# Two-block RWKV-7 and attention layer on one core: key norms and bonus sums spread by DMA

## The chip, the cores and the metric

One core of a Trainium2 chip runs the whole kernel. The metric is the device time of one execution in microseconds (us), lower is better. The time of the kernel before is known from three runs, and one more execution was profiled.

## The reference, cut to what matters

The layer takes x of 512 tokens by 1024 channels. A normed input is multiplied by a wide matrix; from its columns come an RWKV-7 recurrence, a windowed attention and gates, then two projections, an output matrix and a feed-forward block with a short convolution. The change touches the RWKV part alone, in two of its expressions:

```
kk = heads(kf * k_k)
kk = kk / maximum(sqrt(sum(kk * kk, axis=-1)), 1e-12)          # key norms
...
bonus = sum(rh * kh * r_k, axis=-1, keepdims=True) * vh         # bonus sums
y = (groupnorm(y) * lnx_w + lnx_b + bonus) * g
```

Both need a sum over the 64 channels of a head for every token, and then that one number again in all 64 channels.

## The kernel before, in words

Everything is written by hand, one instruction stream for each engine, with semaphores between them. A channel sits in a partition and the 512 tokens run along the row. Sixteen heads go in eight pairs, one pair (n = 0 to 7) filling the 128 partitions; z[:, n] holds r, z[:, n + 8] k and z[:, n + 16] v of pair n. The tokens are four chunks (j) of 128. For each pair TensorE does, in this order:

- scan(n - 1): the state goes over the four chunks of the pair before, and its output lands in bank 6;
- scores(n, n - 1): sixteen 64-row products (L1837) give the chunk matrices; norm_var (L1816) sums the squared output of the pair before over channels with by_row (L1768), four products with 32 columns of weights each that write different 32-row stripes of bank 6; turned_var, deviations and turned (L1776) turn these numbers and spread them over channels; bonus(n - 1) (L1806) multiplies the product r*k in z[:, d + 8] by rkones, a 128x128 matrix of r_k in head blocks, and gives the bonus sum of a head in all its channels in one step;
- invert(n, n - 1) (L1860): seven levels (lv = 0 to 6) that double an inverse of eight 128x128 matrices. A level from 1 on is: PE products L1898 and transposes L1876, DVE masked copies L1355 (v), PE products L1921, DVE sums L1362 (yy), each in two groups. ACT copies the transposed half (L902).

These are short, dependent steps, so PE fills its waits from a table: `fill(place)` runs k-steps of a large fp32r product with the input (three matmuls, L1652 to L1654), "masks" after L1898 and "update" after L1921. Eight steps are one tile of 128 columns of w_in; a pair takes three tiles: FILL = SLOT_A, SLOT_C, SLOT_B (L2010 to L2016). Every tile needs its weights split beforehand in a high part by ACT (L714) and a low part by DVE (L1118, 1024 columns), which DVE does in the levels 1 and 4 of the inversion and at its pair's start.

DVE carries the other pieces of the pair before in the same levels of its own invert (L1332): add_bonus (L1302) at level 2, with_bonus (L1313) and the spreading of the next key norms at level 3, gated (L1318) at level 5. For pairs 0 to 2 fill_low (L1327) is added at levels 3 and 6. scaled_output (L1307) runs ahead of value_tokens (L1252). At its start invert makes xx (L1336) from n1 and the constant first_level, both in SBUF, and level 0 of yy (L1347) follows xx.

The key norms: key_sums (L1782) gathers the sums of all sixteen heads as rows of bank 2, one row for a chunk and head; ACT takes the root into krow (L822); PE turns krow (turned_sums, L1794); DVE takes the reciprocal (L1272). For each pair DVE copies two columns over 64 columns each into kqn (L1279), PE turns kqn (key_norms, L1798), ACT copies it back (L826), and DVE multiplies it in at the start of the next scan (key, L1212).

GpSimd (POOL) has its own queue, in order: the attention's stores, the zeroing of gb and gk, and for each pair bonus_product (L634, r*k of the pair), gate_out (L625, DMA stores), and remainder (L629), which subtracts the two SBUF tensors gb and n1 and is needed at the end of the inversion. kqn lies at the same place as ysq, the spread deviations. SyncE loads weights, each load waiting for the low part three tiles earlier.

Of the kernel before, what the change touches and what calls it, by code (L numbers as in the profile page):

```python
# [36 lines left out]
P = 128  # L37
T = 512
D = 1024
KT = D // P  # L40
# [18 lines left out]

RAW, HL = 4, 2  # L60
# [49 lines left out]
def build(nc, x, norm1_g, w_in, rwkv_mu, w0, w2, a0, a2, g2, k_k, k_a, r_k, lnx_w, lnx_b,  # L110
          b_qkv, attn_sink, gate_b, w_proj_a, w_proj_b, w_out, norm2_g, w_up, conv_w,
          conv_b, w_down, normf_g, out):
    with ExitStack() as ctx:
# [104 lines left out]
        knorm = take("knorm", [P, NT, 2 * PAIRS])  # L218
# [17 lines left out]
        rkones = take("rkones", [P, P])  # L236
        take = taker(KVR, PREP)
# [4 lines left out]
        gk = take("gk", [P, NT, 2, 2 * C])  # L242

# [29 lines left out]
        attn = nc.dram_tensor("attn_scratch", (P, KT, T), F32, kind="Internal").ap()  # L273
        ps = [ctx.enter_context(nc.psum_tensor(f"ps{b}", [P, T], F32)) for b in range(8)]
# [4 lines left out]
        w_hi = sem("w_hi")  # L279
        w_lo = sem("w_lo")  # L280
# [48 lines left out]
        norm_ps = sem("norm_ps")  # L329
        kex_ready = sem("kex_ready")  # L330
        kn_ps = sem("kn_ps")
        kqn_ready = sem("kqn_ready")
# [199 lines left out]
        def _(pool):  # L532
# [125 lines left out]
            for c in (6, 7):  # L658
                attention_out(c)
# [46 lines left out]
        def _(act):  # L706
# [117 lines left out]
            def key_norm_back(n, bank=6):  # L824
                act.wait_ge(kn_ps, n + 1)
                act.activation(kqn[:, :], ps[bank][:, :], ACT.Copy).then_inc(kqn_ready, 1)  # L826

# [66 lines left out]
            def invert(n, d, following):  # L894
# [9 lines left out]
                for lv in range(LEVELS):  # L904
# [11 lines left out]
                    if lv == 5 and following:  # L916
                        key_norm_back(n + 1)
# [34 lines left out]
            for t in range(RKV_TILES):  # L952
# [28 lines left out]
                if t == RKV_TILES - 1:  # L981
                    key_norm_back(0, 2)
# [25 lines left out]
            act.wait_ge(bonus_ps, PAIRS)  # L1008
# [103 lines left out]
        def _(dve):  # L1112
# [93 lines left out]
            def prepare(n):  # L1206
# [5 lines left out]
                def key():  # L1212
                    dve.wait_ge(kqn_ready, n + 1)
# [58 lines left out]
            def key_factors():  # L1272
                dve.wait_ge(norm_ps, 1)
                sums = ps[2][:, P:2 * P].rearrange("p (j h) -> p j h", j=NT)[:, :, 0:2 * PAIRS]
                chain(dve.tensor_scalar(knorm[:, :, :], sums, 1e-12, None, ALU.max))
                chain(dve.reciprocal(knorm[:, :, :], knorm[:, :, :]))

            def key_norms(n):
                dve.tensor_copy(kqn[:, :].rearrange("p (j h v) -> p j h v", j=NT, h=2),  # L1279
                                knorm[:, :, 2 * n:2 * n + 2].unsqueeze(3)  # L1280
                                .to_broadcast([P, NT, 2, HD])).then_inc(kex_ready, 1)
# [20 lines left out]
            def add_bonus(d):  # L1302
                dve.wait_ge(bonus_ps, d + 1)
                dst, bank = (tile(d + 8), 5) if d < PAIRS - 1 else (bp[:, :], 2)
                chain(dve.tensor_tensor(dst, tile(d + 16), ps[bank][:, :], ALU.mult))
# [18 lines left out]
            def weights(n):  # L1324
                split(n, n % RAW, n % HL)

# [5 lines left out]
            def invert(n, d, following):  # L1332
# [7 lines left out]
                for lv in range(LEVELS):  # L1340
# [913 lines left out]
```

## Time and profile before

| | |
|---|---|
| median of 3 runs | 1091.56 us (1091.25 to 1093.53) |
| the profiled execution's own time | 1091.47 us |
| its span on the core | 1089.6 us |
| granted TensorE clock, mean | 0.998 of full speed (2.4 GHz) |
| PE busy | 1072.5 us, 98% |
| DVE busy | 681.1 us, 63% |
| ACT busy | 503.5 us, 46% |
| POOL busy | 99.9 us, 9% |
| DMA | 97.01 MB, 89 GB/s mean |

The profile is of one execution. PE intervals overlap, since matmuls are pipelined: what one costs is the step from its start to the next one's start, not its length. The eight pairs lie between about 225 and 580 us of the span. An idle time in brackets stands before the instruction, with what ended it.

### The profile page before, as it was taken

To read this page: it belongs to the slowest core of one execution; us is meant where nothing else is said; L and a number is where in the kernel's file an instruction comes from. 1 tells how busy PE (TensorE), PEld (TensorE's weight loads), DVE (VectorE), ACT (ScalarE), POOL (GpSimd) and SP (SyncE) were. 2 spreads that over 40 slices of the span, in tenths; PEclk is the share of its full clock that TensorE was granted. 3 is DMA by queue.
4 is the path that set the end of the run, shared out by engine and by line. 5 is a ranking of instruction groups with operands and counts; after the bars stand their busy time and mean duration, and the time that the engine had idled before them with its cause. 6 is when DMAs were issued, how large, how long until landed. Compare 5 with 4: busy or idle time off the path is not lost.

```text
span 1089.6 us, 17946 instructions
## 1 busy us (share of the span) xinstructions
PE 1072.5 (98%) x6737; PEld 847.2 (78%) x6737; DVE 681.1 (63%) x1159; ACT 503.5 (46%) x860; POOL 99.9 (9%) x150
## 2 busy tenths in 40 slices
PE   7999999999999999999999999999999999999997
PEld 6887887777777777777777888888888888888886
DVE  4224655687887878878876445457777776752234
ACT  5426675634534445345443333465555556531122
POOL 8100000120010110111110110100000000000000
PEclk9999999999999999999999999999999999999999
DMA  7632323211101211113242553423333333322221
GB/s 199 154 89 87 96 80 92 74 48 40 40 24 47 78 40 59 59 43 84 80 136 78 155 154 116 135 78 96 96 92 100 88 90 91 96 97 97 97 78 78
DMA packets 154390, 97.01 MB, mean 89 GB/s; under 512 B 30761, under 2 KB 143703, under 8 KB 154327
## 3 DMA queue, kind: packets, MB, share of 16 engines
q1 hardware_dynamic: 148800, 79.72, 25.5%
q0 software_dynamic: 5376, 16.37, 4.7%
q8 instruction: 45, 0.74, 0.3%
q14 instruction: 18, 0.15, 0.0%
q10 hardware_dynamic: 151, 0.04, 0.0%
HBM read 87.71 MB, written 8.39 MB: 88 GB/s over the span
## 4 chain that ended last, share of the span: by engine, by line
PE 94%; DVE 3%; ACT 1%; issue 1%; ACTq 0%; DVEq 0%
PE ps L1696 16%; PE ps L1699 16%; PE ps L1698 16%; PE ps L1652 5%; PE ps L1654 4%; PE ps L1653 4%; PE ps L2213 4%; PE ps L2211 4%; PE ps L2212 4%; PE ps L1837 3%; PE ps L1969 2%; PE ps L1778 2%; PE ps L1990 2%; PE ps L1921 1%; PE ps L1898 1%; PE ps L1876 1%
## 5 line engine op out<-in xcount | busy, mean ns | idle before, releaser
L1118 DVE TENSOR_TENSOR wlo<-raw,whi 128x1024 fp32r<-128x1024 f32 x142 | 173.7, 1223 | 210.4 <-ACT whi L714 138.3
L714 ACT ACTIVATE whi<-raw 128x1024 fp32r<-128x1024 f32 x124 | 131.2, 1058 | 124.3 <-PE ps L1699 120.6
L1696 PE MATMUL ps<-xnh,whi 128*128 128x512 f32 x344 | 135.8, 395 | 0.0
L1699 PE MATMUL ps<-xnh,wlo 128*128 128x512 f32 x344 | 135.7, 395 | 0.0
L1698 PE MATMUL ps<-xnl,whi 128*128 128x512 f32 x344 | 135.7, 395 | 0.0
L1696 PE MATMUL ps<-xh,whi 128*128 128x512 f32 x248 | 99.7, 402 | 1.7 <-DVE xl L1136 1.7
L1699 PE MATMUL ps<-xh,wlo 128*128 128x512 f32 x248 | 97.9, 395 | 0.0
L1698 PE MATMUL ps<-xl,whi 128*128 128x512 f32 x248 | 97.9, 395 | 0.0
L1652 PE MATMUL ps<-xh,whi 128*128 128x512 f32 x184 | 87.0, 473 | 0.0
L1698 PEld LDWEIGHTS ps<-xnl,whi 128*128 128x128 f32 x344 | 64.8, 188 | 15.2
L1696 PEld LDWEIGHTS ps<-xnh,whi 128*128 128x128 f32 x344 | 64.8, 188 | 15.1
L1699 PEld LDWEIGHTS ps<-xnh,wlo 128*128 128x128 f32 x344 | 64.8, 188 | 15.0
L1654 PE MATMUL ps<-xh,wlo 128*128 128x512 f32 x184 | 72.9, 396 | 0.0
L1653 PE MATMUL ps<-xl,whi 128*128 128x512 f32 x184 | 72.2, 392 | 0.0
L902 ACT ACTIVATE xx<-ps 128x256 f16<-128x256 f32 x96 | 32.0, 382 | 79.9 <-PE ps L1876 79.9
L2213 PE MATMUL ps<-wlo,hh 128*128 128x512 f32 x160 | 63.1, 395 | 0.0
L2211 PE MATMUL ps<-whi,hh 128*128 128x512 f32 x160 | 63.1, 394 | 0.0
L2212 PE MATMUL ps<-whi,hl 128*128 128x512 f32 x160 | 63.1, 394 | 0.0
L1696 PEld LDWEIGHTS ps<-xh,whi 128*128 128x128 f32 x248 | 46.6, 188 | 13.9 <-DVE wlo L1118 1.9
L1699 PEld LDWEIGHTS ps<-xh,wlo 128*128 128x128 f32 x248 | 46.6, 188 | 11.1
L1698 PEld LDWEIGHTS ps<-xl,whi 128*128 128x128 f32 x248 | 46.7, 188 | 10.2
L722 ACT ACTIVATE whi<-raw 128x1024 fp32r<-128x1024 f32 x18 | 19.1, 1059 | 73.7 <-PE ps L2213 73.7
(355 smaller groups left out, 2180.1 us busy)
## 6 DMA issues: line engine op xcount, KB each, us to landing
raw<-in_w_in SPq DMA_DIRECT2D x108, 256.0 KB, 3.2
raw<-in_w_up SPq DMA_DIRECT2D x88, 256.0 KB, 3.2
raw<-in_w_down SPq DMA_DIRECT2D x44, 256.0 KB, 2.8
gates_scratch<-gst POOLq DMA_DIRECT2D x16, 256.0 KB, 2.4
raw<-in_w_proj_b SPq DMA_DIRECT2D x16, 256.0 KB, 4.1
raw<-in_w_proj_a SPq DMA_DIRECT2D x16, 256.0 KB, 3.2
gl<-gates_scratch POOLq DMA_DIRECT2D x16, 256.0 KB, 3.1
raw<-in_w_out SPq DMA_DIRECT2D x16, 256.0 KB, 3.1
```

The lines of the kernel that those rows point to most:

```text
L714: act.activation(flat(whi[:, hb]), flat(raw[:, b]), ACT.Copy).then_inc(w_hi, 1)
L1118: dve.tensor_tensor(flat(lo[:, hb]), flat(raw[:, b]), flat(hi[:, hb]).bitcast(F32), ALU.subtract).then_inc(w_lo, 1)
L1652: pe.matmul(o, whi[:, hb, k, :], self.hi(k), start=k == 0, stop=False)
L1653: pe.matmul(o, whi[:, hb, k, :], self.lo(k), start=False, stop=False)
L1654: ins = pe.matmul(o, wlo[:, hb, k, :], self.hi(k), start=False, stop=k == KT - 1)
L1696: pe.matmul(ps[bank][:, :], whi[:, hb, k, :], hi(k), start=first and k == 0, stop=False)
L1698: pe.matmul(ps[bank][:, :], whi[:, hb, k, :], lo(k), start=False, stop=False)
L1699: ins = pe.matmul(ps[bank][:, :], wlo[:, hb, k, :], hi(k), start=False, stop=last and k == kn - 1)
L1837: ins = pe.matmul(ps[SCORE_BANK[f + h]][:, (j - j0) * 2 * C: (j - j0 + 1) * 2 * C], src[hs, j * C:(j + 1) * C], ar[hs, 1 - n % 2, j, :], s ...
L2211: pe.matmul(o, hh[:, u, toks], hi[:, cols], start=u == 0, stop=False)
L2212: pe.matmul(o, hl[:, u, toks], hi[:, cols], start=False, stop=False)
L2213: ins = pe.matmul(o, hh[:, u, toks], lo[:, cols], start=False, stop=last)
```

## The change

The inverse key norms are computed as rows: DVE clamps krow and takes its reciprocal in place (128x128 values), POOL stores the rows once in a scratch tensor in DRAM, and for each pair two DMAs read the row of a head back with a stride of zero over its 64 channels, straight into kqn. turned_sums, the copy L1279, the turns of kqn and ACT's copy L826 go. For pairs 0 to 6 the bonus sums are made in norm_var by a second by_row with rkcols, 32 columns of weights (ACT writes them in the place of rkones), into the upper stripe columns of bank 6; ACT copies them to brow ahead of the root of the variance; POOL stores brow, waits for that store, and issues two DMAs that read the rows back over the channels into z[:, d + 8]. All this stands in POOL's queue between bonus_product and remainder; the load of the next kqn stands behind remainder. add_bonus reads SBUF for both inputs. Pair 7 keeps the old bonus.

On DVE scaled_output goes from ahead of value_tokens to level 2 of the inversion, add_bonus from level 2 to 3, with_bonus from 3 to 4, and the two splits of levels 1 and 4 become halves of 512 columns at levels 1 and 2, and 4 and 5, with a semaphore w_half for tiles that begin before their second half is there. One of the two fill steps at (4, "masks") goes to (4, "update").

```diff
@@ pool @@
+            def by_head(rows, c):
+                return rows.rearrange("(j c) t -> c j t", j=NT)[c:c + 1].to_broadcast([HD, NT, P])
+            def key_norms_in(n):
+                for h in range(2):
+                    pool.dma_start(kqn[h * HD:(h + 1) * HD, :].rearrange("p (j t) -> p j t", j=NT),
+                                   by_head(key_rows, 2 * n + h)).then_inc(kqn_in, 16)
+            def bonus_back(d):
+                pool.wait_ge(std_ready, d + 1)
+                pool.dma_start(bonus_rows, brow[:, :]).then_inc(brow_stored, 16)
+                pool.wait_ge(brow_stored, 16 * (d + 1))
+                for h in range(2):
+                    pool.dma_start(z[h * HD:(h + 1) * HD, d + 8, :]
+                                   .rearrange("p (j t) -> p j t", j=NT),
+                                   by_head(bonus_rows, h)).then_inc(bonus_in, 16)
+            attention_out(6)
+            pool.wait_ge(krow_ready, 1)
+            pool.dma_start(key_rows, krow[:, :]).then_inc(krow_stored, 16)
+            pool.wait_ge(krow_stored, 16)
+            key_norms_in(0)
+            attention_out(7)
...
             pool.memset(zp[:, :], 0.0).then_inc(cleared, 1)
+            key_norms_in(1)
             remainder(0)
...
                     gate_out(3 * n - 1 - FILL_V)
+                bonus_back(n - 1)
                 remainder(n)
+                if n < PAIRS - 1:
+                    pool.wait_ge(rstd_ps, n)
+                    key_norms_in(n + 1)
@@ scalar @@
-            def key_norm_back(n, bank=6):
...
             def deviation(d):
                 act.wait_ge(var_ps, d + 1)
+                if d < PAIRS - 1:
+                    act.activation(brow[:, :], ps[6][:, P:2 * P], ACT.Copy)
...
-                        act.activation(rkones[:, :], headones[:, :], ACT.Copy, scale=pcol("rk", n))\
+                        dst, src = (rkcols, keycols[:, KEY0:KEY0 + P // NT]) if following else \
+                            (rkones, headones[:, :])
+                        act.activation(dst[:, :], src, ACT.Copy, scale=pcol("rk", n))\
@@ vector @@
-                    dve.wait_ge(kqn_ready, n + 1)
+                    dve.wait_ge(kqn_in, 32 * (n + 1))
...
             def key_factors():
-                dve.wait_ge(norm_ps, 1)
...
+                dve.wait_ge(norm_ready, 1)
+                chain(dve.tensor_scalar(krow[:, :], krow[:, :], 1e-12, None, ALU.max))
+                dve.reciprocal(krow[:, :], krow[:, :]).then_inc(krow_ready, 1)
...
             def add_bonus(d):
+                if d < PAIRS - 1:
+                    dve.wait_ge(bonus_in, 32 * (d + 1))
+                    chain(dve.tensor_tensor(tile(d + 8), tile(d + 16), tile(d + 8), ALU.mult))
...
+            def weights_half(n, half):
+                ks = slice(half * KT // 2, (half + 1) * KT // 2)
+                if half == 0:
+                    dve.wait_ge(w_hi, n + 1)
+                last = dve.tensor_tensor(flat(wlo[:, n % HL, ks]), flat(raw[:, n % RAW, ks]),
+                                         flat(whi[:, n % HL, ks]).bitcast(F32), ALU.subtract)
+                last.then_inc((w_half, w_lo)[half], 1)
@@ vector, invert @@
-                    if lv == 1 and d is not None:
-                        weights(N_FILL + 3 * n + 1)
+                    if lv in (1, 2) and d is not None:
+                        weights_half(N_FILL + 3 * n + 1, lv - 1)
                     if lv == 2 and d is not None:
-                        add_bonus(d)
-                    if lv == 3 and d is not None:
-                        with_bonus(d)
+                        scaled_output(d)
                     if lv == 3:
-                        if following:
-                            key_norms(n + 1)
+                        if d is not None:
+                            add_bonus(d)
                         fill_low(3 * n)
                     if lv == 4:
-                        weights(N_FILL + 3 * n + 2)
+                        if d is None:
+                            weights(N_FILL + 2)
+                        else:
+                            with_bonus(d)
+                            weights_half(N_FILL + 3 * n + 2, 0)
                     if lv == 5 and d is not None:
+                        weights_half(N_FILL + 3 * n + 2, 1)
                         gated(d)
...
                 for f in range(6, 8):
                     masked(n, f)
-                scaled_output(n - 1)
                 value_tokens(n)
@@ tensor @@
             def norm_var(d):
...
-                by_row(6, ysq, meancols[:, :]).then_inc(var_ps, 1)
+                last = by_row(6, ysq, meancols[:, :])
+                if d < PAIRS - 1:
+                    pe.wait_ge(rk_product, d + 1)
+                    pe.wait_ge(rk_ready, d + 1)
+                    last = by_row(6, z[:, d + 8, :], rkcols[:, :], P)
+                last.then_inc(var_ps, 1)
...
-                if d is not None:
-                    bonus(d)
...
-                    if lv == 5 and following:
-                        key_norms(n + 1)
...
-            SLOT_C = {(2, "update"): 1, (3, "masks"): 1, (4, "masks"): 2, (5, "masks"): 2,
-                      (5, "update"): 1, (6, "masks"): 1}
+            SLOT_C = {(2, "update"): 1, (3, "masks"): 1, (4, "masks"): 1, (4, "update"): 1,
+                      (5, "masks"): 2, (5, "update"): 1, (6, "masks"): 1}
```

## Rows read from the trace of the kernel before

**Rows 1.** The profile's page: busy shares, and the chain's shares by engine.
```profile
PE 1072.5 (98%) x6737; PEld 847.2 (78%) x6737; DVE 681.1 (63%) x1159; ACT 503.5 (46%) x860; POOL 99.9 (9%) x150
...
PE 94%; DVE 3%; ACT 1%; issue 1%; ACTq 0%; DVEq 0%
```

**Rows 2.** The chain in order of time, pair 5's scores and level 1: start, us, what.
```profile
450.82 0.86 PE ps L1809 x2
...
456.25 1.13 DVE wlo L1118
```

**Rows 3.** Timeline of PE, same pair: start, length, engine, line, operation.
```profile
446.67 0.43 PE L1772 MATMUL ps<-ysq,meancols 128*32 128x128 f32 x8
...
457.77 0.62 PE L1921 MATMUL ps<-v,xx 128*128 128x64 f16 x8 [0.15 <-DVE v L1355]
458.23 0.48 PE L1652 MATMUL ps<-xh,whi 128*128 128x512 f32 x1
...
459.01 0.29 PE L1898 MATMUL ps<-yy,n 128*128 128x64 f16 x4
...
459.49 0.48 PE L1652 MATMUL ps<-xh,whi 128*128 128x512 f32 x1
```

**Rows 4.** Timeline of DVE in the inversion of the same pair.
```profile
452.04 0.68 DVE L1336 TENSOR_TENSOR xx<-n,first_level 128x1024 f16<-128x1024 f16 x1
...
457.30 0.74 DVE L1355 TENSOR_TENSOR v<-ps,level_mask 128x256 f16<-128x256 f32 x2
458.10 0.75 DVE L1362 TENSOR_TENSOR yy<-ps,yy 128x256 f16<-128x256 f32 x2
458.78 0.68 DVE L1305 TENSOR_TENSOR z<-z,ps 128x512 f32<-128x512 f32 x1
459.49 0.76 DVE L1355 TENSOR_TENSOR v<-ps,level_mask 128x256 f16<-128x256 f32 x2
...
462.05 0.43 DVE L1279 COPY kqn<-knorm 128x512 f32<-128x512 f32 x1
...
467.26 0.68 DVE L1321 TENSOR_TENSOR z<-ysb,ps 128x512 f32<-128x512 f32 x1
467.85 0.74 DVE L1355 TENSOR_TENSOR v<-ps,level_mask 128x256 f16<-128x256 f32 x2
```

**Rows 5.** Timeline ahead of the first pair: PE and DVE around its key norms.
```profile
214.88 0.66 PE L1778 MATMUL ps<-ident,kqn 128*128 128x128 f32 x4
...
215.29 0.48 PE L1696 MATMUL ps<-xh,whi 128*128 128x512 f32 x1
...
217.51 0.74 DVE L1214 SCALAR_TENSOR_TENSOR kkn<-z,par,kqn 128x512 f32<-128x512 f32 x1
```

**Rows 6.** Timeline of ACT: the root of the variance, in the same scores.
```profile
447.16 0.37 ACT L856 ACTIVATE yrow<-ps,eps_col 128x128 f32<-128x128 f32 x1 [2.83 <-PE ps L1772]
```

**Rows 7.** Timeline of POOL: its product alone, then in a later pair; DMA issues; remainder.
```profile
217.89 0.84 POOL L623 DMA_DIRECT2D attn_scratch<-q  x1 [13.80 <-DVE q L1441]
...
226.25 1.27 POOL L638 TENSOR_TENSOR z<-z,kmod 128x512 f32<-128x512 f32 x1
...
442.60 2.11 POOL L638 TENSOR_TENSOR z<-z,kmod 128x512 f32<-128x512 f32 x1 [16.35 <-DVE kp L1247]
444.67 0.58 POOL L627 DMA_DIRECT2D gates_scratch<-gst  x1
448.57 2.25 POOL L631 TENSOR_TENSOR n<-gb,n 128x1024 f16<-128x1024 f32 x1 [3.32 <-ACT n L885]
```

**Rows 8.** DVE beside POOL: the split at 442 us; L1219's durations (ns, min/median/max).
```profile
442.37 1.22 DVE L1118 TENSOR_TENSOR wlo<-raw,whi 128x1024 fp32r<-128x1024 f32 x1
...
L1219 DVE TENSOR_SCALAR t<-t x8: 415/416/824, 218.2 to 519.8; 128x512 f32<-128x512 f32 x8
```

**Rows 9.** DMA issues on the page: count, KB each, median us from issue to landing.
```profile
gates_scratch<-gst POOLq DMA_DIRECT2D x16, 256.0 KB, 2.4
...
out<-ot SPq DMA_DIRECT2D x1, 192.0 KB, 2.3
```

More of the change, by code:

```diff
@@ L57 @@
 NEG = -1e30
+KEY0 = 2 * PAIRS * 2 - 2
 RAW, HL = 4, 2
@@ L236, in build @@
         rkones = take("rkones", [P, P])
+        brow = take("brow", [P, P])
         take = taker(KVR, PREP)
@@ L242, in build @@
         gk = take("gk", [P, NT, 2, 2 * C])
+        rkcols = take("rkcols", [P, P // NT])
         yah = at(XHL, "yah", [P, KT, T], F32R)
@@ L273, in build @@
         attn = nc.dram_tensor("attn_scratch", (P, KT, T), F32, kind="Internal").ap()
+        key_rows = nc.dram_tensor("key_scratch", (P, P), F32, kind="Internal").ap()
+        bonus_rows = nc.dram_tensor("bonus_scratch", (P, P), F32, kind="Internal").ap()
         ps = [ctx.enter_context(nc.psum_tensor(f"ps{b}", [P, T], F32)) for b in range(8)]
@@ L328, in build @@
         norm_ready = sem("norm_ready")
[L329 to L332, printed above, removed]
+        krow_ready = sem("krow_ready")
+        krow_stored = sem("krow_stored")
+        kqn_in = sem("kqn_in")
+        brow_stored = sem("brow_stored")
+        bonus_in = sem("bonus_in")
         tanh_ready = sem("tanh_ready")
@@ L1272, in key_factors @@
             def key_factors():
-                dve.wait_ge(norm_ps, 1)
[L1274 to L1281, printed above, removed]
+                dve.wait_ge(norm_ready, 1)
+                chain(dve.tensor_scalar(krow[:, :], krow[:, :], 1e-12, None, ALU.max))
+                dve.reciprocal(krow[:, :], krow[:, :]).then_inc(krow_ready, 1)
             def deviations(d):
@@ L1302, in add_bonus @@
             def add_bonus(d):
-                dve.wait_ge(bonus_ps, d + 1)
-                dst, bank = (tile(d + 8), 5) if d < PAIRS - 1 else (bp[:, :], 2)
-                chain(dve.tensor_tensor(dst, tile(d + 16), ps[bank][:, :], ALU.mult))
+                if d < PAIRS - 1:
+                    dve.wait_ge(bonus_in, 32 * (d + 1))
+                    chain(dve.tensor_tensor(tile(d + 8), tile(d + 16), tile(d + 8), ALU.mult))
+                else:
+                    dve.wait_ge(bonus_ps, 1)
+                    chain(dve.tensor_tensor(bp[:, :], tile(d + 16), ps[2][:, :], ALU.mult))
             def scaled_output(d):
@@ L1638, in _, with __init__ @@
             class Tile:
-                def __init__(self, n, bank, hi, lo, free):
+                def __init__(self, n, bank, hi, lo, free, half=None):
                     self.n, self.bank, self.hi, self.lo, self.free, self.k = n, bank, hi, lo, free, 0
+                    self.half = half
                 def __call__(self, count):
@@ L1648, in __call__ @@
                         k = self.k
+                        if k == 0 and self.half:
+                            pe.wait_ge(w_half, self.half)
+                        if k == (KT // 2 if self.half else 0):
+                            pe.wait_ge(w_lo, n + 1)
                         if k == 0:
-                            pe.wait_ge(w_lo, n + 1)
                             pe.wait_ge(ps_free, self.free)
@@ L1766, in small_products, with by_row @@
                               stop=True).then_inc(lora_ps, 1)
-            def by_row(bank, src, sums):
+            def by_row(bank, src, sums, o=0):
                 for j in range(NT):
                     r = j * (P // NT)
-                    ins = pe.matmul(ps[bank][r:r + P // NT, 0:C], sums, src[:, j * C:(j + 1) * C],
-                                    start=True, stop=True)
+                    ins = pe.matmul(ps[bank][r:r + P // NT, o:o + C], sums,
+                                    src[:, j * C:(j + 1) * C], start=True, stop=True)
                 return ins
@@ L1792, in key_sums @@
                 ins.then_inc(ss_ps, 1)
-            def turned_sums():
-                pe.wait_ge(norm_ready, 1)
-                pe.transpose(ps[2][:, P:2 * P], krow[:, :], ident[:, :]).then_inc(norm_ps, 1)
-            def key_norms(n, bank=6):
-                pe.wait_ge(kex_ready, n + 1)
-                turned(bank, kqn).then_inc(kn_ps, 1)
             def deviations(d):
@@ L2039, in following @@
                         free = N_FILL + (t, t - 2, t - 1)[t % 3] if t else N_FILL - 2
-                        self.tile = Tile(N_FILL + t, FILL_BANK[t % 3], xs(xh), xs(xl), free)
+                        self.tile = Tile(N_FILL + t, FILL_BANK[t % 3], xs(xh), xs(xl), free,
+                                         2 * (t // 3) - 1 if t % 3 == 1 and t > 1 else None)
                     else:
@@ L2095, in _ @@
                     small_products(0, (3, 4))
-                if t == RKV_TILES - 1:
-                    key_norms(0, 2)
-                product(n, t % 2, t % 2, xs(xh), xs(xl), tile_n=n,
-                        ready=(lambda k: turned_sums() if k == 4 else None)
-                        if t == RKV_TILES - 2 else None)
+                product(n, t % 2, t % 2, xs(xh), xs(xl), tile_n=n)
             pe.wait_ge(o_done, 8)
```

15 lines of the change are left out of this document (3 added, 12 removed).

## The prediction

> **What bounds the kernel now.** I read the page first: PE is busy 98% of the span, and the chain that ended last runs 94% over PE and 3% over DVE [rows 1]. So time is saved by work taken off PE, unless something else then ends its waits last. The chain in order of time shows where DVE already does: in a pair the bonus product is on it with 0.86 us, and then the split of level 1 with 1.13 us [rows 2]. The timelines say why. In a level DVE and PE form a loop. From L1921 to L1362 are 0.33 us, L1362's two products take 0.68 until the next piece, and the first half of L1355 (0.38) with 0.09 to PE releases the next L1921: 457.30 + 0.38 + 0.09 = 457.77 [rows 3, 4]. That is 1.48 us plus DVE's pieces. PE's own side is L1921 0.25 (half of the sixteen L1898 and L1876, 459.01 to 459.49), a fill step of 0.78 (458.23 to 459.01), 0.48 and a fill of 0.78: 2.29 us [rows 3]. **Pieces over 0.81 us in a level with two fills stall PE**, and then its second group too, by 0.25 (DVE 0.37 for a group, PE 0.12). The split of 1.13 us does so at level 2: 0.32 + 0.25, some 0.55 us.
>
> **The change part by part,** against the profiled execution's own 1091.5 us, which the median of 1091.56 meets within 0.1. It repeats by pair: 0 is special, 1 and 2 have fill_low, 3 to 6 are plain, 7 has no next one.
>
> *Bonus on PE, pairs 1 to 7.* The product of 0.86 us goes [rows 2]. Four more striped products in norm_var come. The trace has the like: eight records in 0.43 us, of which the last's own length is about 0.28 [rows 3]. So they cost between 0.15 and 0.43, and 0.86 if stripes did not run side by side; I take 0.22, nearest to the row. ACT then does a copy of 128 columns ahead of the root, which took 0.37 [rows 6]; back to back I take 0.2 to 0.27 for it. PE hides that behind the "scores" fill but for 0.1. Gain: 0.86 - 0.22 - 0.1 = 0.55 us a pair.
>
> *Levels, pairs 3 to 6.* A 512-column piece takes 0.59 to its successor (467.26 to 467.85), a chained one 0.71 (458.78 to 459.49) [rows 4]. Level 1: half a split, 0.60, no stall: +0.55. Level 2: half a split and scaled_output, 1.31 against 0.81: 0.50 + 0.25, so -0.75. Level 3 has the gate on PE and stays covered. Level 4: the turn of kqn goes (four transposes, 214.88 to 215.29, some 0.42 [rows 5]), with a short wait behind it: +0.55; with_bonus and half a split, 1.38, are covered by the fill moved to "update" and the two after it. Level 5: half a split and gated, 1.19 against 0.81: 0.38 + 0.25, so -0.6. With 0.55 of the bonus: 0.55 + 0.55 - 0.75 + 0.55 - 0.6 = **0.3 us gained a pair**, 1.2 for four. The copy to kqn, 0.43 long [rows 4], is gone from DVE, but two halves cost 0.07 more than a whole split and scaled_output enters the loop: DVE has become the bound.
>
> *Pairs 1, 2.* fill_low at level 3 meets one fill fewer ahead of L1921: 0.3 lost, so 0. *Pair 7:* no turn of kqn to remove: 0.3 lost. *Pair 0:* the turn (0.42) and the wait for DVE's copy (0.3) go: 0.7 gained. *Ahead of it:* the turn of kqn 0.41 and of krow 0.1: 0.5 gained, if kqn comes in time. krow's root lands near 208.7; clamp and reciprocal of 128 columns about 1.3, store 2.0, two issues 1.3, landing of the second 3: 216.5, a microsecond before L1214 needs it at 217.51 [rows 5]. Later loads of kqn are issued behind remainder, some 20 us ahead of their use: nothing. bonus_in lands about 6 us after the root; add_bonus asks for it 12.8 us after: nothing. In the queue of SP nothing is moved; low halves come up to 2 us later, and its loads are tiles ahead.
>
> These sum to -0.5 - 0.7 - 1.2 + 0.3 = -2.1 us: **1089.4 without the next part.**
>
> *What waits behind the store.* The three DMAs stand ahead of remainder on POOL. Now remainder runs beside copies from PSUM at 448.57, for 2.25 us [rows 7]. Count from the root's end. POOL: 0.09, store L, two issues of 0.62 each (between 0.58 for gates_scratch and 0.84 for eight times 256 bytes a partition [rows 7]), so remainder starts at L + 1.35. DVE: turn and reciprocal 0.4, spread 0.6, two masked copies 1.27, vsum 0.72, vp 0.61: xx at 3.6 (now at 452.04; 0.24 later by ACT and the stripes, 0.71 earlier without scaled_output). L is not in the trace: 256 KB from POOL took 2.4, 192 KB from SP 2.3 [rows 9]. A quarter of it in as many rows lies between 1.7 and 2.3; I take 2.0, since size moves little. **Then remainder starts at 3.35, a quarter microsecond ahead of xx.**
>
> Both read two SBUF tensors, and the trace shows what that does. bonus_product took 1.27 us alone and 2.11 when it began 0.23 us into the split at 442.37: it waited out the 1.22 us [rows 7, 8]. The other way round L1219, 0.416 us seven times, took 0.824 when it began at 218.17 inside POOL's issue of 217.89, which lasted 0.84 [rows 7, 8]. By these rows the later one stands until the earlier ends. xx would end 0.26 + 0.26 us behind remainder (L1219 ended 0.26 behind the issue for 0.42 of work; xx is 0.68 long): 3.35 + 2.1 + 0.52 = 5.97 instead of 4.28, 1.7 us late. Little absorbs it: L1347's second product ends 0.09 before PE comes to L1898. So 1.6 us a pair, seven times: +11.2.
>
> The Trainium skill, SBUF — State Buffer, section Who interferes with whom, says the same more strongly: a DVE instruction with two SBUF inputs contends with a GpSimd instruction that reads SBUF, and whoever starts first holds the ports for its whole instruction. It speaks against putting remainder behind a wait of uncertain length. The Trainium skill, DMA: Bandwidth & Descriptors, section Anatomy of one DMA, puts a POOL-issued DMA at about 2.0 us plus its bytes over 436 KB/us, by its estimate 2.15 us for 64 KB; remainder would then start at 3.5, still 0.1 ahead, and the sum would hardly change.
>
> Sum: 1091.5 - 2.1 + 11.2 = **1100.6 us**.
>
> **The rivals.**
> - *Remainder misses xx (1089.4).* It decides at L = 2.25: above that, xx is first, remainder waits 0.7 us, and runs until about 454.6 where level 1 needs only PSUM inputs; the half split begins near 455.7. For it: the margin is 0.25 us, and the row for 256 KB, 2.4, lies above the point. Against: a quarter of the bytes. Or the pair of readers does not exclude each other in this order; only DVE's other kind of instruction shows it. Chance 0.34; of it 0.19 faster, 0.15 within 0.2%.
> - *Some pairs collide (1094 to 1098).* The margin is as small as a store's scatter. Chance 0.10, slower.
> - *PE stays the bound (1083).* 0.64 x 7 of bonus, 0.42 x 8 of turns: 7.9 us, all kept. For it: PE's 98%. Against: level 2 and 5 above, where DVE's pieces exceed 0.81. Chance 0.08, faster.
> - *It trades evenly (1091.5):* halves dearer than 0.60, stripes at 0.43: each 0.1 a pair. Chance 0.03.
> - *All pairs collide:* 0.45, slower, with its own range 1098 to 1102.5 (L from 1.7 to 2.2 gives 1.3 to 1.8 a pair).
>
> That the work does not leave PE at all can't be: the instructions are gone.
>
> **How the numbers follow.** 0.2% (2.2 us) is about what a measurement of this kernel tells from no change. Faster 0.19 + 0.08 = 0.27; same 0.15 + 0.03 = 0.18; slower 0.45 + 0.10 = 0.55. The range from 1088.0 to 1102.5 holds nearly all of the collision, the mixed cases and most of the rival at 1089.4; it leaves out PE as the bound and the tails.
>
> **What the profile after would show.** Right: remainder starts before L1336; L1336 lasts some 2 us, or starts late; L1898 of level 1 waits for DVE by over a microsecond; pairs repeat every 45.4 us instead of 44.1. The rival: L1336 stays at 0.68 us, remainder comes after it, periods near 43.8. In both, stalls of L1921 at levels 3 and 6 and none at level 2. Wrong altogether: add_bonus or L1214 waiting for a DMA, striped products over 0.8 us, or no stall at levels 3 and 6, which would mean that a half split is cheaper than 0.6 us.

## The result and the profile after

The changed kernel takes 1109.97 us (median of 4 runs, 1108.66 to 1110.44), the kernel before beside it 1091.42: a ratio of 1.0164, 95% interval 1.0151 to 1.0176. So it is slower, as forecast, but by 18.5 us and not by 9; 1109.97 lies above the range that ended at 1102.5.

The profile's page of the changed kernel answers to [rows 1]: the chain that ended last has lost six points of PE and gained five of DVE, and among its lines xx, L1372, stands with 2% (the old L1336).

```profile
span 1108.1 us, 18000 instructions
...
PE 1077.0 (97%) x6746; PEld 848.7 (77%) x6746; DVE 695.0 (63%) x1165; ACT 500.2 (45%) x859; POOL 121.5 (11%) x188
...
PE 88%; DVE 8%; issue 2%; ACT 1%; DMA 1%; SPq 0%; DVEq 0%; ACTq 0%
```

PE is busy 4.5 us *longer* than before, though the bonus products and turns are gone from it. That is the first sign that its own steps have become slower.

The timelines of POOL, DVE and PE in pair 5 (452.74 to 499.90 us) answer to [rows 7], [rows 4] and [rows 3]. Columns: start, length, engine, line, operation, and the idle time before it with its releaser.

```profile
458.35 0.54 POOL L676 DMA_DIRECT2D bonus_scratch<-brow  x1 [2.96 <-ACT yrow L888]
460.43 1.25 POOL L679 DMA_DIRECT2D z<-bonus_scratch  x2 [1.54 <-DMA bonus_scratch<-brow]
461.70 2.15 POOL L637 TENSOR_TENSOR n<-gb,n 128x1024 f16<-128x1024 f32 x1
```

```profile
461.06 0.69 DVE L1289 SCALAR_TENSOR_TENSOR vp<-vsum,ps 128x512 f32<-128x512 f32 x1
461.66 2.75 DVE L1372 TENSOR_TENSOR xx<-n,first_level 128x1024 f16<-128x1024 f16 x1
464.33 1.27 DVE L1383 TENSOR_TENSOR yy<-ps,level_mask 128x512 f16<-128x512 f32 x2
```

```profile
465.07 0.29 PE L1932 MATMUL ps<-yy,n 128*128 128x64 f16 x4 [1.29 <-DVE yy L1383]
465.66 0.29 PE L1932 MATMUL ps<-yy,n 128*128 128x64 f16 x4 [0.30 <-DVE yy L1383]
465.79 0.53 PE L1693 MATMUL ps<-xh,whi 128*128 128x512 f32 x1
466.12 0.63 PE L1694 MATMUL ps<-xl,whi 128*128 128x512 f32 x1
466.54 0.63 PE L1695 MATMUL ps<-xh,wlo 128*128 128x512 f32 x1
466.97 0.65 PE L1955 MATMUL ps<-v,xx 128*128 128x64 f16 x8
```

Two things are to be seen. The collision is there: remainder (L637) starts while xx is at work, and xx takes 2.75 us instead of 0.68; it ends 0.56 behind remainder's end (464.41 against 463.85), and PE stands 1.29 us before level 1 (below, this wait is "the gap"). And behind that gap PE's own steps grow: L1694 takes 0.63 us where it took 0.39, and follows its neighbour by 0.42 instead of 0.23. The granted clock says why. Windows of the changed kernel, from one bonus product of POOL to the next (pairs 1 to 6). Columns: the stretch and its length, the busy time of PE, PEld, DVE, ACT and POOL, the granted clock, the DMA share and GB/s:

```profile
264.60:312.21 47.61, 45.21 (x417) 33.50 (x415) 39.92 (x86) 18.85 (x38) 7.28 (x7) 0.96 0.22 47
312.21:359.84 47.63, 45.26 (x423) 33.77 (x421) 39.27 (x85) 19.27 (x39) 7.84 (x9) 0.96 0.24 52
359.84:407.00 47.16, 44.99 (x423) 33.66 (x421) 37.96 (x83) 19.19 (x39) 8.92 (x10) 0.96 0.26 64
407.00:452.74 45.74, 43.42 (x423) 32.57 (x421) 37.92 (x83) 19.05 (x39) 8.91 (x10) 1.00 0.27 66
452.74:499.90 47.16, 44.99 (x423) 33.56 (x421) 37.93 (x83) 19.11 (x39) 8.88 (x11) 0.96 0.27 64
499.90:547.06 47.16, 44.98 (x423) 33.76 (x421) 37.97 (x83) 22.17 (x42) 10.48 (x14) 0.96 0.37 97
```

Five of the six have 0.96 and one has 1.00. In pair 5 the clock is at 0.50, that is 1.2 GHz, from about 466.1 to 469.5, a microsecond behind the gap, and from 469.5 on at 1.00 again. A plain pair (3 to 6) costs 47.16 us with the fall and 45.74 without: **1.42 us for each fall**. The pair without one, 4, has the longest gap of the six, 1.43 us against 1.29 to 1.33.

Where the 18.5 us of the profiled executions (1108.1 against 1089.6 of span) come from, by the starts of POOL's bonus product; the kernel before takes 44.09 to 44.23 us for a pair:

| stretch | predicted change | measured |
|---|---|---|
| up to pair 1 | -1.2 | -1.31 |
| pairs 1, 2 | +1.6 each | +3.39, +3.40 |
| pairs 3 to 6 | +1.3 each | +3.03, +1.63, +3.07, +3.06 |
| pair 7 and the rest | +1.9 | +2.23 |

The pair whose clock held took 1.63 more, near the 1.3 of the prediction.

### The profile page after: what moved, and what is told of

The parts are those of the page before. It is cut to its first block, busy times and chain, and to the rows that moved or that the text cites. A ratio compares the mean times of both kernels' runs of the same rounds, so it can differ in the third digit from the quotient of the medians.

```text
span 1108.1 us, 18000 instructions
## 1 busy us (share of the span) xinstructions
PE 1077.0 (97%) x6746; PEld 848.7 (77%) x6746; DVE 695.0 (63%) x1165; ACT 500.2 (45%) x859; POOL 121.5 (11%) x188
## 4 chain that ended last, share of the span: by engine, by line
PE 88%; DVE 8%; issue 2%; ACT 1%; DMA 1%; SPq 0%; DVEq 0%; ACTq 0%
PE ps L1737 16%; PE ps L1740 16%; PE ps L1739 16%; PE ps L1693 4%; PE ps L2241 4%; PE ps L2242 4%; PE ps L2240 4%; PE ps L1695 3%; PE ps L1694 3%; PE ps L1875 3%; PE ps L2002 2%; DVE xx L1372 2%; PE ps L2023 2%; PE ps L1955 2%; PE ps L1932 1%
## 5 line engine op out<-in xcount | busy, mean ns | idle before, releaser
L1149 DVE TENSOR_TENSOR wlo<-raw,whi 128x1024 fp32r<-128x1024 f32 x128 | 156.7, 1224 | 211.3 <-ACT whi L748 139.1
L1694 PE MATMUL ps<-xl,whi 128*128 128x512 f32 x184 | 74.0, 402 | 0.0
```

What stands on the lines that cost most here:

```text
L1149: dve.tensor_tensor(flat(lo[:, hb]), flat(raw[:, b]), flat(hi[:, hb]).bitcast(F32), ALU.subtract).then_inc(w_lo, 1)
L1694: pe.matmul(o, whi[:, hb, k, :], self.lo(k), start=False, stop=False)
```

## The experiments

All edits but those named otherwise are on the changed kernel. Lines differ by one or two where an edit adds some.

**Where remainder stands on POOL.** Three orders take the collision away, each by other means. x_start is the semaphore that xx raises when it has ended.

```
e1_ahead                e2_after_xx                          e3_store_late
-  bonus_back(n - 1)       bonus_back(n - 1)                 -  bonus_back(n - 1)
   remainder(n)         +  pool.wait_ge(x_start, n + 1)         remainder(n)
+  bonus_back(n - 1)       remainder(n)                      +  pool.wait_ge(x_start, n + 1)
                                                             +  bonus_back(n - 1)
```

> The changed kernel, with remainder (the POOL subtraction n2) queued ahead of the bonus store and its two reads instead of behind them, pairs 1 to 7. Theory (remainder holds xx, and the gap that this leaves on TensorE is followed by a stretch at the lower clock): remainder then starts near 459, right after ACT's n1, beside copies from PSUM as in the kernel before; xx is 0.7 us long again, TensorE waits under 0.6 us before level 1, the granted clock of a pair is 1.00 instead of 0.96. Pairs repeat every 44 instead of 47.2 us, so 1088 to 1092 us; the upper end if the issue of the store, which then comes just ahead of xx, holds xx by some 0.3 us a pair. Rival 1 (DVE is simply the bound after the change, and what xx waits for has come later by its pieces): xx may be short, but the gap before level 1 stays over 1 us and the time stays above 1104. Rival 2 (the DMAs' own traffic delays DVE or TensorE): stays near 1110.

> The changed kernel with one wait more on POOL: remainder starts only when xx has ended (pairs 1 to 7), store and reads stay ahead of it. Theory (remainder holds xx): xx 0.7 us, remainder from about 462.4 to 464.5 beside products out of PSUM, granted clock 1.00, 1088 to 1091 us. If a POOL subtraction with two SBUF inputs also slows DVE's products of PSUM by an SBUF mask, yy would be longer and the time 1092 to 1100. Rival (DVE's backlog, not remainder, is what holds level 1): no more than 3 us below the changed kernel, above 1104.

> The changed kernel with remainder ahead of the bonus store, and the store waiting until xx has ended: neither remainder nor an issue of a DMA stands beside xx. Theory: 1088 to 1090 us, the lowest of the three orders, since add_bonus asks for the sums 12 us after the store; xx 0.7 us, clock 1.00. Rival (DVE's backlog): above 1104, as in the other two orders. If it is over 1 us below the order with remainder ahead alone, the issues hold xx as well.

Measured: 1090.02, 1090.09 and 1089.88 us, ratios to the kernel before 0.9981 (0.9972 to 0.9991), 0.9986 (0.9976 to 0.9995) and 0.9986 (0.9976 to 0.9996). Each gives back all 18.5 us and a little more; the prediction's sum without a collision was 1089.4. xx is 0.68 or 0.69 us long in all three, and a plain pair of e3_store_late:

```profile
397.14:440.83 43.69, 43.12 (x423) 32.51 (x421) 35.73 (x83) 19.05 (x39) 8.94 (x10) 1.00 0.28 69
```

43.69 against 45.74 with the collision and a full clock: the collision costs 2.05 us a pair, the lower clock 1.42 more. DVE's backlog and the traffic of the reads fall as causes, since both are unchanged here. In e1_ahead the store is issued just ahead of xx, beside vp, and nothing is held by it that can be measured.

e3_store_late was expected to be the lowest of the three; its median is lower by 0.14 us only, which is no difference that can be told. With the store issued so late, add_bonus waits for its sums in pairs 1 and 6, by 0.38 and 0.75 us. These two pairs take 44.55 and 44.29 us, against 44.06 and 43.70 in e1_ahead. The row of DVE in pair 6:

```profile
503.38 0.69 DVE L1331 TENSOR_TENSOR z<-z 128x512 f32<-128x512 f32 x1 [0.75 <-DMA z<-bonus_scratch]
```

**Who wins when they meet.** In the changed kernel xx was recorded ahead of remainder in each of pairs 1 to 7, by 0.04 to 0.17 us, and lost each time. Pair 4 has the widest lead; its rows of DVE and of POOL:

```profile
415.92 2.88 DVE L1372 TENSOR_TENSOR xx<-n,first_level 128x1024 f16<-128x1024 f16 x1
```

```profile
416.09 2.15 POOL L637 TENSOR_TENSOR n<-gb,n 128x1024 f16<-128x1024 f32 x1
```

Here remainder waits for vp, the instruction of DVE ahead of xx.

```
                bonus_back(n - 1)
+               pool.wait_ge(vp_ready, n + 1)
                remainder(n)
```

> The changed kernel, with remainder waiting for vp, the DVE instruction ahead of xx: both become ready within about 0.1 us and xx, which follows vp on its own engine, should be first. In the changed kernel itself xx was recorded 0.04 us ahead of remainder and was held all the same, so which of the two wins at such a distance is open. If the one that starts first holds the other in both directions (the row on which the prediction rested): xx stays at 0.7 us, remainder is recorded at up to 2.8 us, 1089 to 1091 us. If remainder holds xx even when it starts at the same time or after it: xx 2.5 us or more, 1105 to 1112 us. If they share, each longer by half: 1093 to 1098 us.

Measured: 1088.60 us, ratio 0.9975 (0.9965 to 0.9985). The rows of DVE and of POOL, pair 5:

```profile
449.40 0.68 DVE L1373 TENSOR_TENSOR xx<-n,first_level 128x1024 f16<-128x1024 f16 x1
```

```profile
449.57 2.52 POOL L637 TENSOR_TENSOR n<-gb,n 128x1024 f16<-128x1024 f32 x1
```

xx is ahead by 0.17 us and keeps its 0.68; remainder takes 2.52 instead of 2.14, so now it is POOL that waits, at no cost. It holds in both directions that one of the two keeps the other out. The recorded starts don't say which: xx lost with leads of 0.04 to 0.17 us in the changed kernel and of 0.21 in e4_fill_in_gap, and won with 0.17 to 0.25 here. What differs is what remainder starts behind, the issue of a DMA there and the semaphore of vp here; that this is the reason is not shown. (By the Trainium skill, SBUF — State Buffer, section Who interferes with whom, issue order decides who blocks the other: the trace agrees that either can be the one held, with 2.75 us one way and 2.52 the other.)

**The collision alone, with no DMA.** On the kernel before, remainder is made to start beside vp.

```
                chain(dve.tensor_reduce(vsum[:, :], ..., ALU.add))
+               dve.memset(carrier[:, 0:1], 0.0).then_inc(summed, 1)
                dve.scalar_tensor_tensor(vp[...], ...)
...
+               pool.wait_ge(summed, n + 1)
                remainder(n)
```

> The kernel before, with no DMA of the change in it: only remainder is made to wait until DVE has summed the values (a small memset behind vsum signals it), so that it starts some 0.4 us ahead of xx. If remainder beside xx and the gap that follows are the whole cause of the loss: xx about 2.4 to 2.8 us instead of 0.68, TensorE waits 1.3 to 1.8 us before level 1, and the granted clock falls to 1.2 GHz behind it in most pairs. 7 x 1.7 us for the wait and up to 7 x 1.4 us for the clock: 1103 to 1112 us. Without the clock falling (only the wait) 1103. Rival (the loss needs the store, the reads or their traffic): within 3 us of the kernel before.

Measured: 1100.82 us, ratio 1.0091 (1.0074 to 1.0108); plain pairs take 45.40 us, 1.3 more than before.

```profile
456.95 2.26 DVE L1339 TENSOR_TENSOR xx<-n,first_level 128x1024 f16<-128x1024 f16 x1
```

```profile
456.53 2.13 POOL L632 TENSOR_TENSOR n<-gb,n 128x1024 f16<-128x1024 f32 x1 [6.36 <-DVE carrier L1260]
```

xx again ends 0.55 behind remainder (459.21 against 458.66), but remainder began 0.42 ahead instead of beside it, so xx is 1.58 late and PE's gap is 0.69 us. The clock stays at 1.00 in every pair: 7 x 1.3 us, and little more. The collision needs none of the change's DMAs. The fall of the clock that was expected with it did not come, and the time lies 2 us below the lower end expected.

**The fall of the clock.** First the gap is filled, with the collision left as it is.

```
-  (0, "masks"): 2, (1, "masks"): 1, (1, "update"): 1, (2, "masks"): 1}
+  (0, "masks"): 3, (1, "masks"): 1, (1, "update"): 1}
```

> The changed kernel with one fill step of slot A moved from (2, masks) to (0, masks), that is into the gap that TensorE has before level 1; the order on POOL and DVE stays, so xx is still held for about 2.7 us. If the stretch at the lower clock follows from the long gap: the gap shrinks from 1.3 to about 0.5 us, a second wait of up to 0.8 us opens at level 2, the sum of the waits stays, but the granted clock of a pair is 1.00 instead of 0.96, and six pairs give back 1.4 us each: 1100 to 1103 us. Rival (the clock falls for another reason, such as power or the count of products): clock still 0.96 in these pairs, 1108 to 1112 us.

Measured: 1102.45 us, ratio 1.0095 (1.0079 to 1.0112). xx is still 2.8 us long (2.94 in pair 5), the gap in pair 5 is 0.79, a wait of 0.39 opens at level 2, and:

```profile
401.99:447.52 45.53, 43.69 (x423) 32.76 (x421) 37.94 (x83) 19.05 (x39) 8.89 (x10) 1.00 0.27 66
```

One k-step of one product in another place gives back 7.5 us. Then gaps are made in the kernel before by DVE alone: xx is written several times over.

```
+               for _ in range(3):        # e12_xx_three_times: 2, e14_xx_six_times: 5
+                   chain(dve.tensor_tensor(xx, n1, first_level, ALU.mult))
                dve.tensor_tensor(xx, n1, first_level, ALU.mult).then_inc(x_start, 1)
```

> The kernel before, with xx written four times over on DVE (three chained copies of the instruction in front of the real one, some 0.71 us each): no DMA and no work on POOL is moved, only xx ends 2.1 us later, in all 8 pairs. The wait alone: 2.05 us a pair, 16 us, 1108. If the clock falls behind the gap by itself, as after the gaps of 1.3 us in the changed kernel: 1.4 us more in most pairs, 1115 to 1120 us, with 1.2 GHz in the 3 to 4 us behind the gap. If what fell there came from the traffic of the reads or from POOL's subtraction: the clock stays at 2.4 GHz, 1107 to 1109.

> As e11_xx_four_times with two copies in front: xx ends 1.4 us later, TensorE waits about 1.3 us before level 1, the same as in the changed kernel (1.29). The wait alone: 8 pairs by 1.35 us, 10.8 us, 1102. If a gap of this length is enough for the clock to fall, as it was in five of six pairs of the changed kernel: up to 10 us more, 1108 to 1113. If the clock stays at 2.4 GHz: 1101 to 1103, and then the changed kernel's fall needed something beside the gap.

Measured: 1109.06 us (1.0166, 1.0148 to 1.0184) and 1101.90 us (1.0101, 1.0083 to 1.0119). Without a fall a pair takes 46.02 and 45.27 us, 1.9 and 1.2 more than before, near the 2.2 and 1.4 by which xx is later. But the gaps that the rows show are 1.27 and 0.54 us (an idle time in them starts at the modelled end of the last matmul, and the second group of products waits 0.30 more), so e11_xx_four_times, not e12_xx_three_times, is the one like the changed kernel. With 0.54 the clock is 1.00 in all six pairs; with 1.26 to 1.30 it fell in one of six:

```profile
267.91:315.06 47.15, 45.53 (x415) 34.04 (x413) 39.90 (x88) 19.26 (x38) 4.39 (x3) 0.96 0.12 35
```

So such a gap can do it without a collision and without a DMA of the change, but need not. Four more experiments ask what decides.

```
e13_mended_xx_four: e1_ahead, xx four times over      e14_xx_six_times: kernel before, six times
e15_changed_shifted: the changed kernel, +  for _ in range(0 if n else 5):   (pair 0 alone)
e16_xx_four_shifted: kernel before,      +  for _ in range(3 if n else 8):
```

> The changed kernel with remainder ahead of the store (no collision), and xx written four times over on DVE, so that TensorE waits some 1.3 us before level 1. If the clock's fall needs the collision or the traffic beside the gap: 1.00 in the pairs, 44.0 + 1.9 = 45.6 to 46 us each, 1104 to 1106. If it follows from the changed kernel's own TensorE work and the gap: 0.96 in most pairs and 1.4 us more each, 1111 to 1115.

> The kernel before with xx written six times over: the gap on TensorE is 1.42 us longer than with four, about 2.7 us. If length decides, the clock falls in all pairs: 46.0 + 1.4 + 1.4 = 48.9 us each, 1128 to 1132. If the moment decides, only in some of them; without any fall, 47.4 us each, 1120.

> The changed kernel, with xx written six times over in pair 0 alone, so that all later pairs come 2 to 4 us later than they did. If the collision, its traffic or the work decides, the clock falls in the same five pairs by the same amount, 1112 to 1114. If the moment decides, another number of pairs falls: 1104 to 1114.

> The kernel before with xx four times over in pairs 1 to 7 and nine times in pair 0: gaps of 1.27 us as in e11_xx_four_times, all of them some 3.5 us later in time. If the moment decides, the clock can fall in other pairs than there, or in more or fewer of them: 1110 to 1120. If not, it is 3.5 us above e11_xx_four_times, 1112.5, with one pair of six at 0.96.

Measured, two runs each: 1115.87 us (1.0222, 1.0192 to 1.0252), 1129.57 (1.0347, 1.0308 to 1.0387), 1114.99 (1.0214, 1.0159 to 1.0269) and 1113.97 (1.0205, 1.0175 to 1.0234). e13_mended_xx_four, with no collision (remainder ahead, xx never held) and gaps of 1.40 to 1.42 us, has 0.96 in five of pairs 1 to 6: the collision is not needed. In e15_changed_shifted the gaps in pairs 1 to 6 are those of the changed kernel (1.29 to 1.42 us) and come 2.5 to 7 us later in time. In the profiled execution two of the five pairs that fell there fall again, 5 and 6, and pairs 1, 2 and 3 keep their clock:

```profile
409.55:455.29 45.74, 43.44 (x423) 32.56 (x421) 37.90 (x83) 19.06 (x39) 8.89 (x11) 1.00 0.27 66
455.29:502.76 47.47, 45.03 (x423) 33.74 (x421) 37.93 (x83) 19.25 (x39) 8.88 (x11) 0.96 0.26 64
```

e16_xx_four_shifted has the gaps of e11_xx_four_times, later in time, on the kernel before, and pair 2 is hit in place of pair 1. Even gaps of 2.7 us (e14_xx_six_times) left two of six pairs at 1.00. So the length of a gap alone doesn't decide: of those from 1.26 to 2.75 us some were followed by a fall and some not, and none up to 0.79 us was, in the profiled executions.

That the moment decides is not shown by this. The number of falls also differs between executions of one and the same kernel. The other execution of e15_changed_shifted took 1117.51 us at a mean clock of 0.987, the profiled one 1112.47 at 0.992: at 1.42 us a fall, an estimate of three falls more with nothing moved. For the changed kernel it is 1108.66 us at 0.994 against 1109.8 to 1110.44 at 0.991. With one profiled execution of each kernel, the shift can't be told from this variation; besides, it was made by a long gap in pair 0 that was followed by a fall itself.

**The levels.** The prediction's steps at levels 2 and 5 are tested by moving halves of the split, on e3_store_late.

```
e7_half_lv6                                   e8_halves_lv3_lv6: the same, and
   if lv == 5 and d is not None:              -  if lv in (1, 2) and d is not None:
-      weights_half(N_FILL + 3 * n + 2, 1)    -      weights_half(N_FILL + 3 * n + 1, lv - 1)
       gated(d)                               +  if lv == 1 and d is not None:
   if lv == 6:                                +      weights_half(N_FILL + 3 * n + 1, 0)
+      if d is not None:                      ...
+          weights_half(N_FILL + 3 * n + 2, 1)          add_bonus(d)
       fill_low(3 * n + 1)                    +         weights_half(N_FILL + 3 * n + 1, 1)
```

> The changed kernel with the store behind xx (the order of e3_store_late), and the last half of the split of tile 3n+2 moved from level 5 to level 6. It tests the prediction's step at level 5: half a split and gated, 1.19 us against an allowance of 0.81, stall TensorE by 0.6 us a pair at level 6. If so, that stall goes, level 6 takes 0.6 us in an allowance that has no other piece in pairs 3 to 7, and 6 pairs give 0.5 us: 1086 to 1088 us. If DVE's pieces do not set the levels (TensorE is the bound as in the rival at 1083): no change, 1089.5 to 1090.5. If the remainder fill then waits for the late half: 1090 to 1094.

> As e7_half_lv6, and the second half of the split of tile 3n+1 moved from level 2 to level 3, beside the gate on TensorE. It tests the prediction's step at level 2 (half a split and scaled_output, 1.31 against 0.81: 0.5 + 0.25 = 0.75 us a pair): scaled_output alone, 0.6 us, should not stall; level 3 then has 1.31 us behind a gate of 1.10 us and may lose 0.1 to 0.4 us of it, and pairs 1 and 2, with fill_low at level 3, lose what they gain. Net 4 x 0.4 to 0.6 us below e7_half_lv6: 1084 to 1086.5 us. If neither level was set by DVE, 1089.5 to 1090.5.

Measured: 1087.15 us (0.9963, 0.9951 to 0.9976) and 1088.43 us (0.9973, 0.9961 to 0.9984). Moving the half out of level 5 takes 0.54 us off a plain pair, 43.15 against 43.69: the 0.6 of the prediction was there. Moving the other out of level 2 does what was expected at its place (from level 3's first group on PE to level 4's 2.57 us instead of 3.16), but level 3 takes all of it back (the next stretch grows from 2.28 to 2.86): 43.10 us a pair, and pairs 1 and 2, with fill_low there too, lose. Two pieces beside the gate are too many: 1084 to 1086.5 was expected, and e8_halves_lv3_lv6 is not even below e7_half_lv6. Both carry the late store of e3_store_late, and add_bonus waits for its sums in pairs 1 and 6 (0.28 and 0.43 us in e7_half_lv6, 0.51 and 0.95 in e8_halves_lv3_lv6); that is part of the loss.

**The key norms alone**, on the kernel before: store and loads of the key rows as in the change, no turn, no spread, no copy back; the bonus stays on PE.

```
+            key_norms_in(0)          # and (1) ahead of remainder(0), (n + 1) behind remainder(n)
-                        if following:
-                            key_norms(n + 1)        # DVE, level 3
-                    if lv == 5 and following:
-                        key_norms(n + 1)            # PE; and ACT's copy back
```

> The kernel before with the key norms' part of the change alone: rows stored to DRAM once, kqn loaded by broadcasting reads on POOL, no turn, no spread copy, no copy back; the bonus stays on TensorE, splits, scaled_output and fills stay as they were, and nothing stands ahead of remainder. By the prediction's terms: turn of kqn with its short wait 0.55 us in each of pairs 1 to 6, 0.7 in pair 0, 0.5 ahead of the pairs: 4.5 us, so 1087 us. If TensorE has no slack to lose in level 4 only the 0.42 us of the turn counts: 1088. If the copy on DVE was hidden and the turn as well: 1091.5. If the loads of kqn hold an instruction of DVE: over 1091.5.

Measured: 1090.31 us, 0.9987 (0.9978 to 0.9996): faster by 1.3 us, not by 4.5. The start gives its part (pair 1's bonus product comes at 265.13 instead of 265.91), but the pairs give none: 44.10 us as before. The timeline of PE, where the turn stood between level 4 and 5:

```profile
462.36 0.41 PE L1913 MATMUL ps<-v,xx 128*128 128x64 f16 x8
463.17 0.29 PE L1890 MATMUL ps<-yy,n 128*128 128x64 f16 x4 [0.40 <-DVE yy L1367]
```

The turn had stood in a wait for DVE's yy, and that wait of 0.40 us is now empty. What it could be worth together with the fill that the whole change moves to (4, "update"), and with the split cut in halves, no run shows.

**Both mends together:** e7_half_lv6 with the order of e6_beside_xx.

> The changed kernel with both mends: remainder waits for vp, so that it starts just behind xx (the order of e6_beside_xx, which had the lowest time of the three orders), and the last half split sits at level 6 (e7_half_lv6). The two act on different waits, so their gains should add: 1088.6 less the 2.7 us that e7 gained on its own base is 1086 us, range 1085 to 1087.5. If the moved half collides with what follows in this order, it stays at 1087 to 1088.6.

Measured: 1087.73 us, 0.9963 (0.9949 to 0.9977). The sum was expected at 1086, and 1087.73 is no better than e7_half_lv6 alone: the two gains do not add where it can be measured. In the profiled execution they do in part: add_bonus waits nowhere, pairs 1 and 6 take 43.49 and 43.16 us against 43.87 and 43.38, and the span is 0.6 us shorter, within what executions of e9_combined differ by (1086.53 to 1088.29). Either is 0.37% below the kernel before and 2% below the changed one.

## Why the prediction was wrong

**The start** (-1.2 us): right, -1.31. But kqn was not there a microsecond early. DVE waited 0.51 us for the load, and key began at 217.38, where it had begun at 217.51. The broadcasting reads landed 4.7 us behind their issue (median), where 3 had been taken. add_bonus never waited for its sums in the changed kernel.

**Bonus on PE** (0.55 gained): from POOL's bonus product to level 1 e3_store_late takes 10.88 us, the kernel before 11.53: 0.65. The second group of stripes started 0.24 us behind the first, against 0.22 taken.

**Levels**, by the first group of L1898 in each (L1933 in e3_store_late), timelines of pair 5 before and in e3_store_late:

```profile
456.20 0.29 PE L1898 MATMUL ps<-yy,n 128*128 128x64 f16 x4
...
461.46 0.28 PE L1898 MATMUL ps<-yy,n 128*128 128x64 f16 x4
...
464.21 0.29 PE L1898 MATMUL ps<-yy,n 128*128 128x64 f16 x4
...
467.28 0.29 PE L1898 MATMUL ps<-yy,n 128*128 128x64 f16 x4
```

```profile
453.78 0.29 PE L1933 MATMUL ps<-yy,n 128*128 128x64 f16 x4
...
456.07 0.29 PE L1933 MATMUL ps<-yy,n 128*128 128x64 f16 x4
...
459.25 0.28 PE L1933 MATMUL ps<-yy,n 128*128 128x64 f16 x4
...
461.52 0.29 PE L1933 MATMUL ps<-yy,n 128*128 128x64 f16 x4
...
464.60 0.29 PE L1933 MATMUL ps<-yy,n 128*128 128x64 f16 x4
```

| from level | before | e3_store_late | gain | predicted |
|---|---|---|---|---|
| 2 to 3 (DVE's piece in level 1) | 2.81 | 2.29 | 0.52 | 0.55 |
| 3 to 4 (level 2) | 2.45 | 3.18 | -0.73 | -0.75 |
| 4 to 5 | 2.75 | 2.27 | 0.48 | 0.55 |
| 5 to 6 | 3.07 | 3.08 | -0.01 | 0 |
| 6 to the decay product (level 5) | 1.60 | 2.11 | -0.51 | -0.6 |

With the 0.65 that is 0.40 a pair, the 44.10 less 43.69 that was measured, against 0.3. For level 4 the reason given was not borne out: e10_keys_only shows that the turn by itself is worth nothing there, so the 0.48 comes from it only together with what else the change does there, or from the rest alone.

**The store.** L, from the store's issue to the end of the wait for it, was 2.08 us (458.35 to 460.43), against 2.0 taken. By the Trainium skill, DMA: Bandwidth & Descriptors, section Anatomy of one DMA, an estimate of 2.15 had been worked out; the trace agrees within 0.1. What was mis-sized is the small term in front of it: the store was issued 0.30 us behind the root's end (457.69 + 0.36), not 0.09. So remainder stood at 3.65 behind the root, not 3.35, and xx at 3.61 (3.6 had been said). By the prediction's own rule xx then comes first and is not held. It was held in all seven pairs, in pair 4 even with a recorded lead of 0.17 us. The mechanism was the one forecast, but by the prediction's own rule it should have missed with the times that were measured: that it came is luck, and a chance of 0.45 against 0.34 was a fair account of it.

**The size of the collision.** xx ended 0.56 behind remainder (0.52 had been said). As remainder began 0.3 later behind the root, xx came out 2.07 us late instead of 1.7, and a pair lost 2.05 instead of 1.6.

**The step that failed** is the price of the collision, "1.7 us late ... So 1.6 us a pair": it ended with PE's wait. The gap of 1.3 us was followed in five pairs by 3.4 us at 1.2 GHz, 1.42 us each. The sum of the first table's excess over the prediction is 3.6 in pairs 1 and 2, 5.6 in pairs 3 to 6 and 0.3 behind, less 0.1 in front: 9.4 us, just what 1109.97 less 1100.6 is; 5 x 1.42 = 7.1 of it is the clock, the other 2.3 the larger collision, 0.45 a pair, less the 0.1 a pair that the levels and the bonus gave beyond the forecast. Without the falls that is an estimate of 1102.9, against 1102.5 where the range ended. The rows of before could not show this, for in its pairs PE has no such gap; but the prediction priced a gap on PE at its length and did not ask what may follow it, and the range had nothing in it for that.

The rivals: the one without a collision, 1089.4, is what e1_ahead, e2_after_xx and e3_store_late are, within 0.7 us. PE as the bound (1083) is excluded by the levels. What stays open is what decides whether the clock falls behind a gap, and why e6_beside_xx came out 1.3 to 1.5 us below the other orders. For e3_store_late the two waits of add_bonus are part of it. For e2_after_xx the profiled executions show nothing: 1088.66 us against 1088.95 in e6_beside_xx.

## What to carry to other kernels

Count a gap on TensorE as more than its length: here one shown as 1.3 us cost 2.05 by itself and 3.5 with the clock behind it, and the same kernel with one k-step of independent work put into each gap was 7.5 us faster. An instruction of GpSimd that reads SBUF and has 20 us to spare should never be queued behind a wait whose end falls near a short VectorE instruction with two SBUF inputs on the path; order it ahead of the wait, or tie it to that instruction by a semaphore. And before work is priced as saved, look whether it stands in a wait that remains without it.

## What the runs showed of the hardware that was not expected

- Behind a gap of 1.26 to 1.43 us on a TensorE that was busy for about 95% of a pair, the granted clock can fall to 0.50 (1.2 GHz) and come back 3.4 us later. In the profiled executions 5 of 6 pairs fell, or 2 of 6, or 1 of 6, with gaps of the same length. Gaps of 0.54 to 0.79 us in the pairs were never followed by a fall.
- Between xx and remainder the recorded starts don't tell who holds whom: xx lost with leads of 0.04 to 0.21 us and won with 0.17 to 0.25. The one held, xx, ends 0.54 to 0.57 us behind the other for 0.68 us of work, so little of its work can have been done before.
